# A first merge block as seven products, a second one ahead of a compression block, and later table transfers

## The reference, cut to what matters

```
h    = rms_norm(x, norm_mix)
cols = h @ w_in            # queries, keys, values of three attentions, gate logits, forget logits, 'merge' (3 x 1024)
o_a, o_b, o_c = nsa_mixer(cols), swa_mixer(cols), fox_mixer(cols)
gates = sigmoid(cols['merge']).reshape(b, t, 3, 1024)
x = x + (gates * (branches @ w_branch)).sum(axis=2) @ w_out
x = x + conv_ffn(rms_norm(x, norm_ffn))
```

## Time and profile before

| | us |
|---|---|
| median of 3 runs | 1607.23 |
| lowest, highest | 1605.67, 1608.98 |
| the profiled execution's own time | 1613.06 |
| its span | 1611.3 |
| TensorE busy in it | 1589.4 |
| VectorE, GpSimd, ScalarE busy | 657.0, 506.1, 401.4 |

### The profile page before, as it was taken

How to read it: one execution, slowest core, us unless ns; L and a number is a source line. 1 busy time by engine, 2 the same in 40 slices (tenths; PEclk the granted TensorE clock), 3 DMA queues, 4 the chain that set the end, 5 groups by cost and what they waited for, 6 DMA issues and landing times.

```text
span 1611.3 us, 18886 instructions
## 1 busy us (share of the span) xinstructions
PE 1589.4 (99%) x7203; PEld 1009.2 (63%) x7203; DVE 657.0 (41%) x1605; ACT 401.4 (25%) x1058; POOL 506.1 (31%) x504
## 2 busy tenths in 40 slices
PE   8999999999999999999999999999999999999999
PEld 3874555468356448884464767558645444788854
DVE  2634344434322534763565424244522323222254
ACT  2104444321243211011452225311233320100000
POOL 1524554132153122520351316447422210010051
PEclk9999999999999999999999999999999999999999
DMA  9452230422440323224522521256533223344441
GB/s 346 185 209 106 97 157 1 163 89 75 172 177 9 130 88 123 87 97 158 208 81 105 192 104 67 73 156 163 197 114 151 105 77 132 151 143 146 146 181 68
DMA packets 23176, 210.73 MB, mean 131 GB/s; under 512 B 3160, under 2 KB 7960, under 8 KB 10672
## 3 DMA queue, kind: packets, MB, share of 16 engines
q1 hardware_dynamic: 19440, 195.74, 32.4%
q0 software_dynamic: 3648, 13.79, 3.0%
HBM read 204.75 MB, written 1.49 MB: 128 GB/s over the span
## 4 chain that ended last, share of the span: by engine, by line
PE 94%; DMA 2%; DVE 1%; POOL 1%; ACT 1%; issue 0%; SPq 0%; DVEq 0%; ACTq 0%
PE bank L739 27%; PE bank L1237 14%; PE bank L1593 9%; PE bank L883 5%; PE bank L897 5%; PE bank L1619 4%; PE bank L1532 4%; PE bank L870 3%; PE bank L1125 3%; PE bank L1115 2%; PE bank L1149 2%; PE bank L801 2%; PE bank L752 2%; PE bank L1140 1%; DMA ring<-stream 1%; PE bank L1106 1%
## 5 line engine op out<-in xcount | busy, mean ns | idle before, releaser
L739 PE MATMUL bank<-ring,arena 128*128 128x512 f32 (+2 forms) x864 | 357.1, 570 | 1.0 <-DVE arena L1679 1.0
L739 PEld LDWEIGHTS bank<-ring,arena 128*128 128x128 f32 x864 | 161.9, 190 | 176.5 <-issue 165.2
L3138 POOL TENSOR_SCALAR arena<-arena,stat 128x512 f32<-128x512 f32 (+1 forms) x128 | 168.0, 1325 | 177.0 <-DVE stat L1825 176.8
L1593 PE MATMUL bank<-arena,ring 128*128 128x256 f32 (+1 forms) x768 | 152.8, 362 | 0.0
L1593 PEld LDWEIGHTS bank<-arena,ring 128*128 128x128 f32 x768 | 136.0, 190 | 17.0 <-issue 0.5
L2715 ACT ACTIVATE arena<-arena,stat 128x513 f32<-128x513 f32 (+3 forms) x128 | 81.3, 636 | 126.1 <-DVE stat L1817 126.0
L1237 PE MATMUL bank<-arena 128*128 128x256 f32 x432 | 96.4, 379 | 0.0
L897 PE MATMUL bank<-ring,arena 128*128 128x512 f32 x192 | 89.6, 602 | 2.0 <-DMA ring<-stream 1.1
L883 PE MATMUL bank<-arena,ring 128*128 128x512 f32 (+1 forms) x256 | 90.5, 497 | 0.3 <-DVE arena L1801 0.2
L1237 PEld LDWEIGHTS bank<-arena 128*128 128x128 f32 x432 | 81.9, 190 | 11.9 <-issue 0.8
L1237 PE MATMUL bank<-arena,ring 128*128 128x256 f32 x384 | 85.4, 380 | 0.0
(11 more groups left out here) (372 smaller groups left out, 2289.6 us busy)
## 6 DMA issues: line engine op xcount, KB each, us to landing
ring<-stream SPq DMA_DIRECT2D x87, 2048.0 KB, 8.0
ring<-stream SPq DMA_DIRECT2D x6, 1024.0 KB, 9.9
arena<-arena POOLq DMA_DIRECT2D x50, 64.0 KB, 3.0
gate_rows<-gate_scratch POOLq DMA_DIRECT2D x3, 1024.0 KB, 4.8
masks_sb<-masks POOLq DMA_DIRECT2D x2, 1024.0 KB, 5.1
arena<-g_scratch POOLq DMA_DIRECT2D x1, 2048.0 KB, 10.7
arena<-rev_scratch POOLq DMA_DIRECT2D x8, 256.0 KB, 7.4
ring<-stream SPq DMA_DIRECT2D x1, 1536.0 KB, 7.2
```

The costliest lines, as they stand in the source:

```text
L739: last = mm(dst, a, b, start=(k == 0), stop=(k == len(pairs) - 1))
L1593: last = mm(ps[:, SEQ * part + cols.start:SEQ * part + cols.stop], w[:, a:a + P], hT2[:, k, cols], start=(k == 0), stop=(k == DC - 1))
L3138: nc.gpsimd.tensor_scalar(row, row, stat[:, 3, s:s + 1], None, ALU.mult).then_inc(w_norm, 1)
```

## The change

- m0 is made by seven products, as a seventh block of `small_products` (b = 6). Products 0 to 3 stand between the fifth and the sixth turn `s qkT`, products 4 to 6 behind the tenth.
- The results are added up by VectorE into the place of the merge gates, and ScalarE then applies the tanh there in place, four times on 128 x 256. A new flag `first_merge_ready` tells VectorE's first branch save of it.
- GpSimd makes three more sums of 128 x 1024 (`small_differences(6)`) behind the roots `rest`.
- The last pair of table transfers moves from ahead of the roots `main 0` to between the roots `main 1` and `rest`.
- In the stream m1 stands ahead of cmp_v, and in the planner's list `hid 1` stands behind merge product 2. By the planner's costs, steps 1 and 2 then hold the first seven matmuls of product 2, step 3 its eighth and `hid 1`. From step 4 on the steps are as before.
- TensorE's `wait_saved(pe, "s small quads")` ahead of `attend_branches` now stands for seven blocks.

```diff
-SMALL = ("p1", "p2", "p3", "p4", "p5", "p6")
+SMALL = ("p1", "p2", "p3", "p4", "p5", "p6", "m0")
...
-    blocks += [("s m0", BLOCK), ("s cmp_k", BLOCK), ("s cmp_v", BLOCK), ("s m1", BLOCK), ("s cmp_w2", 4 * DIM2)]
+    blocks += [("s m0", BLOCK), ("s cmp_k", BLOCK), ("s m1", BLOCK), ("s cmp_v", BLOCK), ("s cmp_w2", 4 * DIM2)]
...
-    items = [("cum", 0, 1.1), ("hid", 0, 1.9), ("cumT", 0, 1.2), ("hid", 1, 1.9)] + merge(2)
-    items += [("hidT", 0, 0.0), ("hidT", 1, 0.6), ("cmp begin", 0, 0.0)] + merge(3, 0, 4) + [("cmp", 0, 1.0)] + merge(3, 4)
+    items = [("cum", 0, 1.1), ("hid", 0, 1.9), ("cumT", 0, 1.2)] + merge(2)
+    items += [("hid", 1, 1.9), ("hidT", 0, 0.0), ("hidT", 1, 0.6), ("cmp begin", 0, 0.0)] + merge(3, 0, 4) + [("cmp", 0, 1.0)] + merge(3, 4)
...
                 if i == BEFORE_BRANCHES:
-                    merge_products(0, range(DC))
+                    small_products(6, range(4))
                 turn_group(g, [qk[:, t, rows(c)] for c in QK_TURNS[i] for t in range(LT)])
-            merge_products(1, range(DC))
+            small_products(6, range(4, 7))
             wait_saved(pe, "s small quads")
...
             save("s qkT", turned_qk, range(0, BEFORE_BRANCHES))
-            for w in range(2):
-                save_windows(w)
-            save("s qkT", turned_qk, range(BEFORE_BRANCHES, 10))
+            def between(place):
+                if place == "second":
+                    save_windows(0)
+                elif place == "third":
+                    save("s qkT", turned_qk, range(BEFORE_BRANCHES, 10))
+                    save_windows(1)
+            combine_small(6, between)
...
-            save_merge(0)
+            save_small(6)
             save("s qkT", turned_qk, range(BEFORE_BRANCHES, 10))
-            save_merge(1)
+            for i, (t, n) in enumerate(((0, 0), (1, 1), (0, 1), (1, 0))):
+                if i < 3:
+                    sc.wait_ge(small_v, 36 + (1, 5, 6)[i])
+                else:
+                    wait_saved(sc, "s small quads")
+                at = small_target(6, t, n)[0]
+                last = act_op(at, at, ACT.Tanh, scale=0.5)
+            last.then_inc(flag("first_merge_ready"), 1)
...
             for b in range(1, 5):
                 small_differences(b)
-                for a in range(2 * SKEWED * (b - 1), 2 * SKEWED * b, SKEWED):
-                    pool.dma_start(bias[a:a + SKEWED], ...).then_inc(flag("bias_in"), 16)
+                if b < 4:
+                    bias_rows(b)
             root_of_heads("main 0")
             small_differences(5)
             root_of_heads("main 1")
+            bias_rows(4)
             root_of_heads("rest")
+            small_differences(6)
```

More of the change, by code:

```diff
@@ L223, in group_stages @@
     out += [("s rev", "v"), ("s p", "v"), ("s hT", "va"), ("s p", "a"), ("s small quads", "v" * 5), ("s small logits", "v"), ("s small", "v"),
-            ("s zT", "va"), ("s small quads", "v"), ("s qkT", va(BEFORE_BRANCHES)), ("s m0", "a"), ("s qkT", va(10)[BEFORE_BRANCHES:]), ("s m", "a")]
+            ("s zT", "va"), ("s small quads", "v"), ("s qkT", va(10)), ("s small quads", "v")]
     owners = {"cum": "v", "hid": "a", "cumT": "v", "hidT": "a", "cmp begin": "v", "cmpT": "v", "sc": "v", "pT": "va", "m": "a", "br": "v"}
@@ L660, in second_inputs, with small_sums_before @@
             return [(qk[:, i, 0:HALF], ps[:, :], None, None)]
+        def small_sums_before(b):
+            return 3 * b - (b > 5)
         def small_target(b, t, n):
+            if SMALL[b] == "m0":
+                return [merge[0][t][:, SEQ * n:SEQ * n + SEQ]]
             c, at = 1 + b, HALF * (1 + b) + SEQ * n
@@ L678, in build @@
         small_token_sums = [XN[:, HALF * i:HALF * (i + 1)].rearrange("p (k n) -> p k n", n=P) for i in range(4)]
-        small_sums = [thirds(r) for r in (V, Z)]
+        small_sums = [thirds((V, Z)[i % 2]) for i in range(6)] + [[quarter(r) for r in (HT[:, 2048:3072], HT[:, 3072:4096], Z[:, 3072:4096])]]
         small_first, small_total, small_other = (probs[:, i, 0:SEQ] for i in range(3))
@@ L890, in merge_products @@
             def merge_products(j, chunks):
-                g = STAGES["s m"][j - 1] if j else STAGES["s m0"][0]
+                g = STAGES["s m"][j - 2]
                 if chunks[0] == 0:
@@ L1507, in small_products @@
                 w, g = weights(f"s {SMALL[b]}").rearrange("p (k n) -> p k n", k=DC), STAGES["s small quads"][b]
-                t1, t2, t4 = small_sums[b % 2]
+                t1, t2, t4 = small_sums[b]
                 s1, s2, s3, s4 = small_token_sums
@@ L1518, in small_products @@
                         pe.wait_ge(flag("small_tokens_ready"), 1)
-                        pe.wait_ge(small_sums_made, 3 * b + 2)
+                        pe.wait_ge(small_sums_made, small_sums_before(b) + 2)
                     elif i == 3 and b:
@@ L1523, in small_products @@
                         pe.wait_ge(small_a, b + 1)
-                        pe.wait_ge(*((flag("last_small_difference"), 1) if b == 5 else (small_sums_made, 3 * b + 3)))
+                        pe.wait_ge(*((flag("last_small_difference"), 1) if b == 5 else (small_sums_made, small_sums_before(b) + 3)))
                     elif i == 5:
@@ L1937, in save_branch @@
                     wait_saved(dve, "s m")
+                    dve.wait_ge(flag("first_merge_ready"), 1)
                 dst = merged[:, t, cols] if m == BRANCH_ORDER[0] else branch_tmp
@@ L2484, in combine_small @@
                 add([small_total], 2, small_first, 0).then_inc(small_v, 1)
-                t1, t2, t4 = small_sums[b % 2]
-                dve.wait_ge(small_sums_made, 3 * b + 2)
+                t1, t2, t4 = small_sums[b]
+                dve.wait_ge(small_sums_made, small_sums_before(b) + 2)
                 vec_op.tensor_tensor(t4, part_of(small_weights(b), 0, 1), t2, ALU.subtract).then_inc(flag("small_last_ready"), 1)
@@ L2764, in save_merge @@
             def save_merge(j):
-                ps = wait_made(STAGES["s m"][j - 1] if j else STAGES["s m0"][0])
+                ps = wait_made(STAGES["s m"][j - 2])
                 t, c = j % 2, j // 2
@@ L3213, in small_differences @@
                 nc.gpsimd.tensor_tensor(t1, part_of(w, 1, 0), part_of(w, 0, 0), ALU.subtract).then_inc(small_sums_made, 1)
-                pool.wait_ge(small_sums_made, 3 * b + 1)
+                pool.wait_ge(small_sums_made, small_sums_before(b) + 1)
                 nc.gpsimd.tensor_tensor(t2, part_of(w, 1, 1), t1, ALU.subtract).then_inc(small_sums_made, 1)
-                if b < 5:
+                if b != 5:
                     nc.gpsimd.tensor_tensor(part_of(w, 1, 0), part_of(w, 1, 1), part_of(w, 1, 0), ALU.subtract).then_inc(small_sums_made, 1)
@@ L3225, in root_of_heads, with bias_rows @@
                 nc.gpsimd.tensor_tensor(heads(rstd), heads(rstd), heads(power), ALU.pow).then_inc(flag("roots_done"), 1)
+            def bias_rows(b):
+                for a in range(2 * SKEWED * (b - 1), 2 * SKEWED * b, SKEWED):
+                    pool.dma_start(bias[a:a + SKEWED], bass.AP(scratch.tensor, P - 1 - a, [[16 * 384 - 1, SKEWED], [384, 16], [1, SEQ]]))\
+                        .then_inc(flag("bias_in"), 16)
             small_differences(0)
@@ L3231, in _ @@
                 small_differences(b)
-                for a in range(2 * SKEWED * (b - 1), 2 * SKEWED * b, SKEWED):
-                    pool.dma_start(bias[a:a + SKEWED], bass.AP(scratch.tensor, P - 1 - a, [[16 * 384 - 1, SKEWED], [384, 16], [1, SEQ]]))\
-                        .then_inc(flag("bias_in"), 16)
+                if b < 4:
+                    bias_rows(b)
             root_of_heads("main 0")
```

## The result

The changed kernel takes 1623.64 us in the median (1621.89 to 1624.67, 4 runs) against 1606.45 (1605.64 to 1608.98, 4 runs) of the kernel before: 1.0096 times as long, 95% interval 1.0079 to 1.0113. The medians differ by 17.2 us; the ratio stands for 15.4 us (12.7 to 18.2 by its interval). Forecast were 4 to 5: the sign was right, the size was not, and the time lies outside the range.

A forecast was written before the change was run, and what follows sets the result against it. TensorE, busy 1589.4 of 1611.3 us, was taken as the bound. Terms A to F summed to +2.8 us against the profiled execution; with A at -5.8, +3.8 on 1607.23 gave 1611.0 us, range 1605.0 to 1616.0.

The forecast's parts named there:

- A: p6's products: with the table transfers moved, the gap and the half clock behind it go, -6.8 us; -5.8 for timed runs.
- B: Behind p6's products: TensorE newly waits for VectorE's last normalised heads, +0.5 us (0 to 1.3).
- C: m0: seven products of 1.73 us replace two tiles, 13.8 us together, -1.7 us (-1.7 to 0).
- D: Start of the attention: first scores wait until VectorE has saved m0's last product, +0.6 us (0.4 to 1.0).
- E: Merge product 2: m1 is loaded in time and its 1.06 us wait goes, -0.8 us (-1.06 to 0).
- F: Merge product 4, step 6: m2 waits for m1's slot, 8.0 us gap plus half clock, +11.0 us (9 to 11.5).
- GpSimd's roots don't join in: Within B: `rest` is shifted 1.12 us later by the two transfers but begins some 6 us earlier with t2.
- m2's load would be hidden: Rival at step 6: m2's load does not stop TensorE, sum -7.2 us, 1600.0 us; chance 0.1.
- p6 late in the changed kernel: Rival at p6's products: its load is slow by itself, A and B are 0, 1616.3 us; chance 0.08.
- the gap would be cheap: Rival at m2's gap: clock soon back or not falling, F 8.0 to 9.5 us, 1608 us; chance 0.27.

The follow-up runs named there:

- experiment 5: Experiment 4's kernel, with GpSimd waiting for the last normalised heads before it makes m0's weight sums: 1608.48 us, ratio 1.0011 to the kernel before.
- experiment 7: The kernel before, with three unused 128 x 1024 differences added on GpSimd behind the roots `rest`: 1611.94 us, ratio 1.0032.
- experiment 6: Experiment 4's kernel, with the last pair of table transfers issued behind m0's weight sums: 1611.78 us, ratio 1.0021 to the kernel before.
- experiment 1: The kernel before, profiled once more unchanged: 1611.66 us, against a median of 1607.40 in 20 runs.
- experiment 3: The kernel before, with only m1 ahead of cmp_v in the stream and hid 1 behind merge product 2: 1616.63 us, ratio 1.0060.
- experiment 2: The kernel before, with only the last pair of table transfers moved to between the roots `main 1` and `rest`: 1608.21 us, ratio 1.0002.
- experiment 4: The changed kernel, with stream order and hid 1 put back as before: 1612.50 us, ratio 1.0031 to the kernel before.
- experiment 12: The kernel before, with m0's first token tile ahead of TensorE's wait for the heads and hid 1's planner cost at 2.3: 1608.55 us, ratio 1.0012.

## Why the prediction was wrong, point by point

Against the profiled execution of before the steps can be read off the two traces:

| step | forecast | measured |
|---|---|---|
| A, p6's gap and its half clock | -6.8 | -7.0 (20.0 to 13.0) |
| B, the wait for the heads | +0.5 | +9.0 |
| C, m0 as seven products | -1.7 | -1.7 |
| D, the wait for the last addition | +0.6 | +0.7 |
| E, m1 in time | -0.8 | -1.1 |
| F, m2 late | +11.0 | +10.2 |
| ahead of p6 | 0 | -1.2 |
| sum | +2.8 | +8.9 |

The spans differ by 8.8. B measured: 6.7 from the end of p6 (1148.11) to the first turn (1154.80), 1.8 by which the turns are longer at half clock (3.95 against 2.13) and 0.5 in m0's first two products. F: 8.0 and what the attention's steps 6 and 7 are longer.

- **B is the step that failed**: +0.5 forecast, +9.0 measured. It has two faults. The first is "GpSimd's roots don't join in". They did: the forecast let them move with t2 at their old length, but they took 14.2 us instead of 8.5. 1.2 of the difference are the two transfers, and 4.6 lie in three instructions beside which VectorE ran one with two SBUF inputs (2.15 for 0.23, 6.28 for 5.44, 2.04 for 0.20). So the gap is 2.24 us even without a sum beside the normalisations (experiment 5). The second fault is larger. The forecast saw that VectorE's instructions lengthen GpSimd's and did not ask the opposite. m0's sums were new work on GpSimd at the moment at which VectorE made the last thing that TensorE waited for. The sums held VectorE for 4.3 us (experiment 7 shows this without any other edit, experiments 5 and 6 in the changed kernel). Behind the gap of 6.53 us the clock was 0.50, which cost 2.3 us more; behind those of 2.24 and 2.70 (experiments 5 and 1) it was 1.00.
- **A was right for the profiled execution and wrong for the runs.** This is the second step that failed: the sum counts -5.8 for the runs, and they show about 0. The forecast had seen the sign of it (5.8 us between the profiled execution and the median) and took it for a question of the fallen clock alone: the gap itself it counted in every run. But of 79 timed executions of the kernel before only ten took over 1610.5 us, and both of its traces are such. Experiment 3's trace has no such gap, and experiment 2 moves the transfers and gains nothing: it guards against the slow load, but the two transfers now stand between the roots, and its turns wait 1.96 us where experiment 3's wait 0.34.
- **Against an execution of before near its median the account fits.** The changed kernel starts the attention at 1174.16, 5.8 us behind experiment 3's 1168.36, and E and F add 9.1 by the table. These 14.9 us stand beside 15.4 (12.7 to 18.2) by the ratio. Experiment 4 starts it at 1174.02, 5.7 us behind, and is 5.1 us above the kernel before. The match is good to about 2 us only, as p6's own start varies from trace to trace, whatever the kernel (1134.80 to 1136.85 in thirteen, 1138.76 in one). The medians' 17.2 us hold 1.75 more, by which the changed kernel's profiled execution is below its own median; no trace shows these. That B to F of the table sum to +17.1, beside 17.2, is luck: against experiment 3's trace B is 0.6 less, and p6 starts 1.5 us sooner.
- **F held** in place, cause and size: 8.03 us gap, half clock behind it, 9 us alone (experiment 3, E included) and 11.1 taken back (experiment 4). The half clock cost 2.2 us instead of 3.0. The 2 us between 9 and 11 are within the intervals.
- **C and D held.** But seven products save little here: 1.7 less 0.7. They need 7.5 us more of GpSimd (2.33, 2.54 and 2.67) at the busiest place.
- **Rivals.** That m2's load would be hidden did not happen; nor was p6 late in the changed kernel. That the gap would be cheap is refuted by experiment 3.
- **The chances** do not add up as described: 0.27 and a quarter of 0.55 are 0.41 and not 0.38, which leaves 0.49 for slower and not 0.52.

## What to carry to other kernels

When work is moved onto GpSimd, look at which VectorE instructions with two SBUF inputs fall beside it, and whether TensorE waits for one of them. In a ring of three blocks, swapping two loads changes which block waits for which slot: write out for each block who had its slot before. And ahead of pricing a gap, compare the profiled execution's own time with the median: to close a gap that few executions have brings the median nothing.

## What the runs showed that I had not expected

- GpSimd's 128 x 1024 sums held VectorE's instructions with two SBUF inputs until a sum ended: 128 x 384 from 0.5 to 2.7 us, 128 x 2048 from 2.28 to 4.49 (experiment 6), 128 x 16 from 0.17 to 1.67 and 1.89 (experiment 5). Beside GpSimd's roots (5.47 us on 128 x 32) VectorE's weight sum kept its 1.22 us.
- p6's load of 2048 KB took 12.0 to 13.9 us with two table transfers of 256 KB issued 0.5 to 1.3 us ahead of it, 10.0 with 3.0 us between, 7.9 and 8.7 with 4.9, and 7.7 to 8.9 with the pair moved, in eight executions.
- The stretch of work at 1.2 GHz behind a gap had no order with the gap's length: 3.1 us behind 2.9 (experiment 12), 6.0 behind 3.8 (before), 4.9 behind 6.5 and 4.1 behind 8.0 (changed kernel), 4.6 behind 8.1 (experiment 3).
